# Four sums over a head in rounded part and remainder, and the request states read in the opening of a pair

## The reference, cut to what matters

```
kk = heads(k * k_k)
kk = kk * lax.rsqrt(jnp.maximum(jnp.sum(kk * kk, axis=-1, keepdims=True), 1e-24))      # sum 1
...
def step(S, inp):
    sa = einsum('bhij,bhj->bhi', S, a_t)
    S = S * w_t + sa[..., None] * b_t + v_t[..., None] * k_t
    return S, einsum('bhij,bhj->bhi', S, r_t)
S_fin, ys = lax.scan(step, wkv_prev, seq)
...
mean = jnp.mean(y, axis=-1, keepdims=True)                                             # sum 2
var = jnp.mean(jnp.square(y - mean), axis=-1, keepdims=True)                           # sum 3
y = ((y - mean) * lax.rsqrt(var + GN_EPS)) * lnx_w + lnx_b
bonus = jnp.sum(r_h * k_h * r_k, axis=-1, keepdims=True) * v_h                         # sum 4
out = (y + bonus) * g
```

## Time and profile before

| | |
|---|---|
| median of 3 runs | 1778.01 us (1776.01 to 1780.81) |
| the profiled execution | 1776.88 us, of which the span from first to last instruction is 1775.3 us |
| PE busy | 99% of the span |
| DVE, ACT, POOL busy | 63%, 43%, 3% |
| granted clock of TensorE | mean 0.996 of full speed |
| one pair in the loop, period | 44.19 us (the start of a tail to the start of the next) |

### The profile page before, as it was taken

The page is one execution under the profiler, slowest core; times in us unless marked ns, Lnnn a source line. Parts: engine busy times, 40 slices in busy tenths (PEclk is TensorE's granted clock), DMA queues, the critical chain, the costliest instruction groups (busy, mean ns, idle before and its releaser), DMA issues.

```text
span 1775.3 us, 40657 instructions
## 1 busy us (share of the span) xinstructions
PE 1758.8 (99%) x16482; PEld 1708.2 (96%) x16482; DVE 1120.7 (63%) x2015; ACT 759.6 (43%) x1059; POOL 53.8 (3%) x103
## 2 busy tenths in 40 slices
PE   9999999999999999999999999999999999999997
PEld 9999899999999998999999999999999999999997
DVE  7764864667777777665566666666666665444443
ACT  6456444555555554333443333333333333333332
POOL 2500000000000000000000000000000000000000
PEclk9999999999999999999999999999999999999998
DMA  7644344433333332644454444444444444555553
GB/s 285 220 165 165 124 162 157 143 115 118 112 112 117 112 111 103 220 166 170 171 220 163 157 164 158 168 161 167 164 165 165 165 165 167 172 169 175 170 169 134
DMA packets 51697, 283.47 MB, mean 160 GB/s; under 512 B 7248, under 2 KB 11856, under 8 KB 25776
## 3 DMA queue, kind: packets, MB, share of 16 engines
q1 hardware_dynamic: 43488, 260.32, 41.9%
q10 hardware_dynamic: 3888, 12.59, 1.9%
q0 software_dynamic: 4256, 9.65, 1.8%
HBM read 274.26 MB, written 8.27 MB: 159 GB/s over the span
## 4 chain that ended last, share of the span: by engine, by line
PE 96%; DVE 3%; DMA 0%; ACT 0%; issue 0%; DVEq 0%; ACTq 0%
PE bank L621 30%; PE bank L623 28%; PE bank L622 28%; PE bank L945 1%; PE bank L985 1%; DVE w_lo L567 1%; DVE scores L1939 1%; PE bank L642 0%; PE bank L643 0%; PE bank L644 0%; DMA w_raw<-in_w_in 0%; PE bank L905 0%; DVE max L1906 0%; PE bank L852 0%; PE bank L800 0%; PE bank L817 0%
## 5 line engine op out<-in xcount | busy, mean ns | idle before, releaser
L621 PE MATMUL bank<-x_split,w_lo 128*128 128x288 f32 x2880 | 872.8, 303 | 2.8 <-DVE w_lo L567 2.1
L622 PE MATMUL bank<-x_split,w_hi 128*128 128x288 f32 x2880 | 849.6, 295 | 0.0
L623 PE MATMUL bank<-x_split,w_hi 128*128 128x288 f32 x2880 | 847.2, 294 | 0.0
L587 ACT ACTIVATE w_hi<-w_raw 128x2048 fp32r<-128x2048 f32 (+1 forms) x262 | 468.7, 1789 | 591.8 <-PE bank L623 579.1
L567 DVE TENSOR_TENSOR w_lo<-w_raw,w_hi 128x2048 fp32r<-128x2048 f32 (+1 forms) x238 | 503.8, 2117 | 283.2 <-ACT w_hi L587 282.9
L621 PEld LDWEIGHTS bank<-x_split,w_lo 128*128 128x128 f32 x2880 | 540.3, 188 | 18.0 <-issue 8.2
L622 PEld LDWEIGHTS bank<-x_split,w_hi 128*128 128x128 f32 x2880 | 541.0, 188 | 2.6 <-issue 1.5
L623 PEld LDWEIGHTS bank<-x_split,w_hi 128*128 128x128 f32 x2880 | 542.2, 188 | 0.0
L621 PE MATMUL bank<-act_split,w_lo 128*128 128x288 f32 x704 | 208.5, 296 | 0.0
L622 PE MATMUL bank<-act_split,w_hi 128*128 128x288 f32 x704 | 207.7, 295 | 0.0
L623 PE MATMUL bank<-act_split,w_hi 128*128 128x288 f32 x704 | 207.0, 294 | 0.0
(11 more groups left out here) (396 smaller groups left out, 1544.2 us busy)
## 6 DMA issues: line engine op xcount, KB each, us to landing
w_raw<-in_w_up SPq DMA_DIRECT2D x88, 1024.0 KB, 4.8
w_raw<-in_w_in SPq DMA_DIRECT2D x47, 1024.0 KB, 4.9
w_raw<-in_w_down SPq DMA_DIRECT2D x64, 704.0 KB, 4.1
w_raw<-in_w_gate SPq DMA_DIRECT2D x32, 1024.0 KB, 4.8
w_raw<-in_w_p SPq DMA_DIRECT2D x16, 1024.0 KB, 4.9
w_raw<-in_w_o SPq DMA_DIRECT2D x16, 1024.0 KB, 4.8
h<-in_x ACTq DMA_DIRECT2D x1, 2304.0 KB, 11.2
h_spill<-h ACTq DMA_DIRECT2D x1, 2304.0 KB, 9.3
```

The lines of the kernel that those rows point to most:

```text
L587: actv(WHI[:, slot, 0:kt], WRAW[:, slot, 0:kt], ACT.Copy).then_inc(sem("w_hi"), 3 if isinstance(n, int) and n == 2 else 1)
L621: mm(out, wl, hi, start=first and k == ks[0], stop=False, skip_group_check=True)
L622: mm(out, w, lo, start=False, stop=False, skip_group_check=True)
L623: ins = mm(out, w, hi, start=False, stop=last and k == ks[-1], skip_group_check=True)
```

## The change

The four sums no longer take one float32 matmul each. The summand is rounded to float32r, the remainder is taken, and two float32r matmuls with rounded ones (`HONES`) add up in the same bank (`head_sum`). Rounding and remainder are new instructions: for sums 1 and 3 a second ACT square that writes a float32r tile and a DVE subtraction, for sum 2 an ACT copy and a DVE subtraction, for sum 4 a DVE cast and a DVE subtraction. `kk_sum` stands ahead of the mean of y; the fills behind the mean and ahead of the bonus are 6 and 5 blocks, not 4 and 6. The reading of the request states stands in the opening, behind the 64 x 32 tiles, and the waits for `bonus` and `sin_in` with it. The requests' states are added on DVE ahead of the last chunk's state. The last chunk's map has a tile of its own (`MT3`). At the start PE issues the products of the first two blocks' rounded weights ahead of those with the weights' remainder, and ACT and DVE split two tiles of x ahead of the first weights.

```diff
+                        if s == 0 and u == 0:
+                            pe.wait_ge(sem("w_part_hi"), 1)
+                            for k in range(2):
+                                pe.wait_ge(sem("x_split"), k + 1)
+                                mm(out, WHI[:, 0, k], XN[:, 0, k], start=k == 0, stop=False, skip_group_check=True)
+                                mm(out, WHI[:, 0, k], XN[:, 1, k], start=False, stop=False, skip_group_check=True)
...
+            def head_sum(bank, split):
+
+                mm(BK[bank][:, 0:N], HONES[:], split[:, 1, :], start=True, stop=False, skip_group_check=True)
+                return mm(BK[bank][:, 0:N], HONES[:], split[:, 0, :], start=False, stop=True, skip_group_check=True)
+
             def kk_sum(v):
-                pe.wait_ge(sem("kk_sq"), v)
-                mm(BK[3][:, 0:N], head_ones, SQK[:], start=True, stop=True).then_inc(sem("kk_sum"), 1)
+                pe.wait_ge(sem("kk_sq"), 2 * v)
+                head_sum(3, SQS).then_inc(sem("kk_sum"), 1)
...
+                pe.wait_ge(sem("bonus"), v)
+                pe.wait_ge(sem("sin_in"), v * 16)
+                settle(pe)
+                for r in range(2):
+                    for g, q in enumerate(quads):
+                        for e, h in enumerate(halves):
+                            mm(BK[(4, 7)[e]][q, 256 + r * HD:256 + (r + 1) * HD], ARS[h, r].rearrange("p x n -> p (x n)"), SIN[h, 4 * r + g, :],
+                               start=True, stop=True)
...
-                pe.wait_ge(sem("bonus"), v)
-                settle(pe)
...
-                pe.wait_ge(sem("sin_in"), v * 16)
                 pe.wait_ge(sem("mats"), v)
                 settle(pe)
...
-                pe.wait_ge(sem("y"), v)
-                pe.wait_ge(sem("y_cols"), v)
-                mm(BK[5][:, 0:N], head_ones, YS[:], start=True, stop=True).then_inc(sem("y_mean"), 1)
                 if not last:
+                    pe.wait_ge(sem("y_cols"), 2 * v - 1)
                     kk_sum(it + 2)
-                fill(4)
-                pe.wait_ge(sem("y_sq"), v)
-                mm(BK[5][:, 0:N], head_ones, YQ[:], start=True, stop=True).then_inc(sem("y_var"), 1)
+                pe.wait_ge(sem("y"), 3 * v - 1)
+                head_sum(5, YSS).then_inc(sem("y_mean"), 1)
+                fill(6)
+                pe.wait_ge(sem("y"), 3 * v)
+                head_sum(5, YSS).then_inc(sem("y_var"), 1)
                 if not last:
                     log_decay(it + 2)
-                fill(6)
+                fill(5)
...
+            first_hi(0, 2, "x_in0")
             act.wait_ge(sem("w_first_in"), 16)
             first_weights(0, [0])
-            first_hi(0, 2, "x_in0")
...
-                actv(SQK[:], RKV[:, 1, :], ACT.Square, scale=PRM[:, PR_KK:PR_KK + 1]).then_inc(sem("kk_sq"), 1)
+                for dst in (SQK[:], SQS[:, 0, :]):
+                    ins = actv(dst, RKV[:, 1, :], ACT.Square, scale=PRM[:, PR_KK:PR_KK + 1])
+                ins.then_inc(sem("kk_sq"), 1)
...
+                act.wait_ge(sem("y"), 3 * v - 2)
+                act.wait_ge(sem("y_cols"), 2 * v - 1)
+                actv(YSS[:, 0, :], YS[:], ACT.Copy).then_inc(sem("y_cols"), 1)
...
-                actv(YQ[:], YS[:], ACT.Square).then_inc(sem("y_sq"), 1)
+                for dst in (YQ[:], YSS[:, 0, :]):
+                    ins = actv(dst, YS[:], ACT.Square)
+                ins.then_inc(sem("y_sq"), 1)
...
+            def kk_lo(v):
+
+                dve.wait_ge(sem("kk_sq"), 2 * v - 1)
+                V.tensor_tensor(SQS[:, 1, :], SQK[:], SQS[:, 0, :].bitcast(F32), ALU.subtract).then_inc(sem("kk_sq"), 1)
...
-                V.scalar_tensor_tensor(RKR[:], RKV[:, 0, :], PRM[:, PR_RK:PR_RK + 1], KP[:], ALU.mult,
-                                       ALU.mult).then_inc(sem("rkr"), 1)
+                st.done(V.scalar_tensor_tensor(RKR[:], RKV[:, 0, :], PRM[:, PR_RK:PR_RK + 1], KP[:], ALU.mult, ALU.mult))
+                st.done(V.tensor_copy(RKS[:, 0, :], RKR[:]))
+                V.tensor_tensor(RKS[:, 1, :], RKR[:], RKS[:, 0, :].bitcast(F32), ALU.subtract).then_inc(sem("rkr"), 1)
...
+                if not last:
+                    kk_lo(it + 2)
                 dve.wait_ge(sem("y_mm"), v)
                 V.tensor_copy(YS[:, SEQ:N], BK[5][:, 384:416]).then_inc(sem("y"), 1)
...
+                dve.wait_ge(sem("y_cols"), 2 * v)
+                V.tensor_tensor(YSS[:, 1, :], YS[:], YSS[:, 0, :].bitcast(F32), ALU.subtract).then_inc(sem("y"), 1)
...
                 if not last:
                     kk_max(it + 2)
+                dve.wait_ge(sem("y_sq"), v)
+                V.tensor_tensor(YSS[:, 1, :], YQ[:], YSS[:, 0, :].bitcast(F32), ALU.subtract).then_inc(sem("y"), 1)
                 for part in range(2):
                     split_part(dve, n + 3, 1, part)
...
+            st.done(V.tensor_copy(HONES[:], head_ones))
+            kk_lo(1)
             streamed(FILL_FIRST)
```

More of the change, by code:

```diff
@@ L398, in build @@
     RKR = m("r_k_rk", [P, N])
+    RKS = m("r_k_rk_split", [P, 2, N], F32R)
+    YSS = m("y_split", [P, 2, N], F32R)
+    assert m.at <= inv_at + 3 * size_of([P, 4, CH])
+    SQS = region(r0)("squares_k_split", [P, 2, N], F32R)
     m = region(big)
@@ L631, in first_units @@
                     for u in range(FIRST):
+                        out = BK[first_bank(u)][:, 0:N]
+                        if s == 0 and u == 0:
[4 more added lines that the diff above has]
+                                mm(out, WHI[:, 0, k], XN[:, 1, k], start=False, stop=False, skip_group_check=True)
                         if s < 2 and u < 3:
@@ L635, in first_units @@
                             pe.wait_ge(sem("w_split"), s + 1)
-                        out = BK[first_bank(u)][:, 0:N]
-                        for k in range(4):
+                        if s == 0 and u == 0:
+                            for k in range(2):
+                                mm(out, WLO[:, 0, k], XN[:, 0, k], start=False, stop=False, skip_group_check=True)
+                        for k in range(2 if s == 0 and u == 0 else 0, 4):
                             t = 4 * s + k
@@ L874, in bonus_mm @@
                 pe.wait_ge(sem("rkr"), v)
-                mm(BK[4][:, 0:N], head_ones, RKR[:], start=True, stop=True).then_inc(sem("bonus_mm"), 1)
+                head_sum(4, RKS).then_inc(sem("bonus_mm"), 1)
             def pair(it, last=False):
@@ L912, in pair @@
                             mm(BK[5 + e][q, tt * P:tt * P + BL], BT[h, c0:c0 + BL], AR[h, 0, c0:c0 + BL], start=True, stop=True)
+                quads = [slice(g * BL, (g + 1) * BL) for g in range(4)]
+                pe.wait_ge(sem("bonus"), v)
[6 more added lines that the diff above has]
+                               start=True, stop=True)
                 for tt, par in chunks:
@@ L935, in pair @@
                 settle(pe)
-                tr(BK[4][:, 288:416], BKV[:].rearrange("p x n -> p (x n)"), ident).then_inc(sem("k_mm"), 1)
+                tr(BK[4][:, 384:512], BKV[:].rearrange("p x n -> p (x n)"), ident).then_inc(sem("k_mm"), 1)
                 fill(5)
-                quads = [slice(g * BL, (g + 1) * BL) for g in range(4)]
                 def blockwise(bank, lhs, rhs, both=False):
@@ L970, in pair @@
                 ins.then_inc(sem("l2s_mm"), 1)
[L971 to L975, removed]
                 for tt in range(2):
@@ L1512, in pair @@
                 for rows in (slice(0, 2 * NS), slice(2 * NS, P)):
-                    actv(TOKS[rows, 0, :], BK[4][0:2 * NS, 288:416], ACT.Copy)
-                actv(TOKS[NS:2 * NS, 1, :], BK[4][P - NS:P, 288:416], ACT.Copy).then_inc(sem("toks_sb"), 1)
+                    actv(TOKS[rows, 0, :], BK[4][0:2 * NS, 384:512], ACT.Copy)
+                actv(TOKS[NS:2 * NS, 1, :], BK[4][P - NS:P, 384:512], ACT.Copy).then_inc(sem("toks_sb"), 1)
                 if not last:
@@ L2230, in pair @@
                 state(0)
[L2231 to L2236, removed]
+                for c, src in ((1, BK[7][:, P:P + CH]), (2, BK[6][:, P + CH:2 * P])):
+                    for e, h in enumerate(halves):
+                        V.tensor_tensor(MTB[h, c - 1, e * HD:(e + 1) * HD], src[h], eye_ch[h], ALU.add)
+                V.tensor_tensor(MT3[:], BK[7][:, P + CH:2 * P], eye_ch, ALU.add).then_inc(sem("map"), 1)
                 rv = AR[:, 1, :].rearrange("p (c f) -> p c f", f=CH)
@@ L2247, in pair @@
                         mix_prev(it + 1, 0)
+                    if c == 3:
+                        dve.wait_ge(sem("state_s_mm"), v)
+                        for r in range(2):
+                            half = SIN[:, 4 * r:4 * r + 4, :]
+                            ins = V.tensor_tensor(half, half, BK[(5, 2)[r]][:, 0:256].rearrange("p (b f) -> p b f", f=HD), ALU.add)
+                        ins.then_inc(sem("s_grown"), 1)
                     dve.wait_ge(sem("state_mm"), v * 3 - 3 + c)
                     state(c)
-                dve.wait_ge(sem("state_s_mm"), v)
```

(6 more changed lines are left out.)

15 lines of the change are left out of this document (9 added, 6 removed).

## The result

The changed kernel takes 1789.79 us (median of 4 runs, 1788.73 to 1790.36); the kernel before takes 1777.04 us (median of 4, 1776.01 to 1780.81) on the same chip. The ratio is 1.0072, with a 95% interval from 1.0060 to 1.0084: slower, by 12.75 us, where 1772.5 us was forecast. The span of its profiled execution is 1788.8 us, against 1775.3.

What follows compares the result with a forecast made beforehand. PE, busy 99% of the span, was taken as the bound. Against the profiled 1776.88 us: -6.54 (sums), -0.7 (states), +1.03 and +0.66 (uncovered places), a net 5.55 off the 1778.01 median: 1772.5 us, range 1770.3 to 1775.6.

Steps and rivals of the forecast that it cites:

- The sums: Head sums on PE: two float32r matmuls for one float32 save 0.218 us each, 6.54 us for 30 sums.
- What is added on DVE: DVE in a pair's tail: new work makes it 1.6 to 1.65 us late against 1.72 allowed, so hidden; booked 0.
- All else that DVE owes keeps its distance: DVE behind L2104: `WLO` still ends near 405.4, ahead of PE's first fill near 405.8, so no stall.
- the 0.1 that the prediction took off: DVE's reciprocal in the tail: it already waited for a root on ACT, so 0.1 us less delay.
- The rival "slower than before": DVE's tail before the transposes: stall above 1.54 us a pair makes it over 0.3% slower; 1.6 gives 1783.7 us; chance 0.03.
- the margin of `ar_ready`: Ahead of the transposes at L905: DVE may be 1.72 us late before PE has to wait.
- The rival of DVE's tail: DVE's tail ahead of the transposes comes out of hiding: 0.25 us a pair, 1774.3 us; chance 0.28.
- The states: Their reading moved to the opening: one tile-size change less, 0.09 us a pair, 0.7 in all; wait for `bonus` hidden.
- The two uncovered places: Last pair's mean and first `kk_sum`, with nothing to hide the added steps: cost 1.03 and 0.66 us.
- The start: First weight products: PE starts over a microsecond earlier, but the second unit still waits for its weights; worth 0.
- The rival that the clock stays up: At the start, earlier PE products prevent the 1.2 GHz stretch, gaining 1.0 us: 1771.5 us; chance 0.14.

Runs made afterwards that it cites:

- both corrections: Changed kernel with the quarters of `w_lo` ahead of the bonus product on DVE and the states read behind the inversion's fourth step again: 1772.07 us, ratio 0.9980.

## Why the prediction was wrong

**The sums** were right. The mean's two matmuls and the block behind them start at 439.97, 440.10 and 440.23 in the changed kernel, 0.13 us apart. With the waits away the period falls by 44.19 - 43.27 = 0.92 us, where 0.87 was booked for four sums; whether the other 0.05 is theirs is not shown.

```profile
439.97 0.29 PE L877 MATMUL bank<-y_split,head_ones_r 128*128 128x288 f32 x1
440.10 0.30 PE L878 MATMUL bank<-y_split,head_ones_r 128*128 128x288 f32 x1
440.23 0.30 PE L627 MATMUL bank<-x_split,w_lo 128*128 128x288 f32 x1
```

**What is added on DVE** was sized right and followed to the wrong places. Counted from the start of the tail's first sum, which is 0.27 us ahead of the mean in the changed kernel, the first two quarters start 0.95 us later than before, as booked, and the last two another 0.83, where 0.8 was booked; the cast takes 0.31 us, the value taken; the reciprocal is 1.6 us later, as added up. `ar_ready` stayed hidden by the tenth of a microsecond that was forecast: it is there at 451.23, the transposes start at 453.26, and without the 1.84 us of the wait ahead of them 0.19 is left, less the 0.07 for the semaphore. PE waits nowhere at L925.

The step that failed is the sentence "All else that DVE owes keeps its distance: after L2104 the whole `WLO`...", by which the tail was booked at 0. It looked at what DVE owes behind `head` and passed over what it owes inside the tail: the quarters at L579, between which the new work was put. The rows for the check stood in the trace of before, with the prediction's own terms. The margin is 0.75. DVE is 0.95 + 0.8 = 1.75 later; the 0.1 that the prediction took off belongs to the reciprocal, which had waited for a root, and not to the quarters. PE is 3 x 0.218 = 0.65 earlier, for the fourth sum stands behind the block. That gives 1.75 + 0.65 - 0.75 = 1.65 us a pair, and 7 x 1.65 = 11.6 us: 1784 us for the forecast's 1772.5, slower than before. The rest up to 1789.8 is mostly that a wait costs more than its idle time (1.84 us a pair), the states, and the first `kk_sum`.

The rival "slower than before" had the right size (a stall above 1.54 us) and the wrong place; it asked for twice what I added up, because it measured from the margin of `ar_ready` and not from the nearest one. The rival of DVE's tail looked at the transposes too. PE's own saving makes every margin in the tail smaller, and I took it off for `ar_ready` and for the first fill of the opening, and not for the blocks of the tail itself.

**The states** failed in both their halves. What I took for a saved change of tile size is still there: L993 to L999 takes the 0.21 us that L969 to L974 took the earlier trace rows, though there is one change of tile size less. And "hidden" was claimed for the wait for `bonus`, when not the wait but the 0.43 us of the states themselves held up DVE's chain. Booked: a gain of 0.7 us; measured with nothing else changed: 8 x 0.45 = 3.6 us lost, 3.9 by the medians.

**The two uncovered places.** The first `kk_sum` shows 0.59 us of idle time and starts 0.76 us behind its place in the stream, where 0.66 was booked. On top of it comes another 0.7 us on the `w_lo` (L573) behind the remainder on DVE, which was not booked; the stretch is 1.3 us longer. The last mean shows 0.58 us and starts 0.75 behind its place, not 0.98. In the changed kernel PE also waits 0.34 and 0.48 us on L585 in the last pair, and what lies behind the last period is 1.5 us longer than before; with both corrections it is 0.6, where 1.03 was booked.

**The start.** Worth 0 within the scatter, as forecast. The rival that the clock stays up fell: PE's first weight product starts at 7.47 us, PE works up to 9.71 and stands idle from there to 11.52, and the granted clock shows 0.50, the level of 1.2 GHz, from 12 to 15 us, where it did from 10 to 13 before (one of these windows is in the earlier trace rows). So the stretch at the low level moved, and did not go. The two products, and a window of the changed kernel (columns as in the earlier trace rows):

```profile
7.47 0.40 PE L643 MATMUL bank<-x_split,w_hi 128*128 128x288 f32 x1 [1.43 <-ACT w_hi L1277]
...
9.42 0.29 PE L659 MATMUL bank<-x_split,w_hi 128*128 128x288 f32 x1
11.52 0.40 PE L657 MATMUL bank<-x_split,w_lo 128*128 128x288 f32 x1 [1.80 <-DVE w_lo L1803]
```

```profile
12.00:13.00 1.00, 1.00 (x6) 1.00 (x5) 1.00 (x3) 1.00 (x4) 0.00 (x0) 0.50 0.80 327
```

**The account.** In the profiled executions the changed kernel is 13.5 us later: 7 x 1.36 in the loop, of which 7 x 1.84 from the tail's wait, 7 x 0.45 from the states' move, and 7 x 0.92 back from the sums (1.84 + 0.45 - 0.92 = 1.37); 1.3 ahead of the loop, 1.5 behind it with the last pair, and 1.1 within the scatter at the start.

## What to carry over

Work that is put into a helper engine's queue delays everything behind it there: list each later item of that queue with the block of the main engine that needs it and the margin between them, and take from every margin both the helper's delay and what the main engine itself gains. Let the smallest margin decide, and place new work behind what has the least; here the same instructions in another order were worth 13 to 14 us. Small products that are moved ahead of a helper's chain hold up the whole chain: what they free at their old place comes back as a wait at the next block that the helper feeds, unless that block has margin.

## What was new about the hardware

- A cast of 288 columns from float32 to float32r within SBUF took DVE 0.31 us, where a subtraction of the same size took 0.46. The Trainium skill (VectorE: DVE Perf Modes, What auto-detection actually checks) lets a one-source instruction with both ends in SBUF run at twice the rate in float32 too; the cast agrees.
- A wait costs PE more than the idle time shown. The block at 446.50 has 1.57 us of idle time. By starts, L629 before it stands at 444.63, so 1.87 us passed instead of 0.13, and the matmul behind it came after 0.24 us (446.74) instead of 0.13: 1.74 + 0.11 = 1.85 us lost, which is the 1.84 of the period. The profile counts idle time only from the modelled end of L629, 0.29 us after its start, while the next matmul would have started after 0.13.
- Four products of 32 x 32 hold PE for 0.21 us whether products of 64 x 32 (414.55 to 414.76) or of 64 x 64 follow (464.36 to 464.57 in the changed kernel).
